# The first half of an output projection as seven half-size products, and the branch products ahead of it in another order

## What is computed

```python
y_a = diff_attention(...)                 # 256 x 512
y_b = gated_delta_net(...)                # 256 x 512
merged = (sigmoid(m_gate_a) * (y_a @ w_branch_attn)    # 512 x 1024
          + sigmoid(m_gate_b) * (y_b @ w_branch_gdn))
x = x + merged @ w_out                    # 1024 x 1024
h2 = rms_norm(x, norm_ffn_gain)
x = x + hier_moe(h2, ...)                 # 32 experts, all weights are read
return rms_norm(x, norm_final_gain)
```

## Time and profile before

| | us |
|---|---|
| median of 3 runs | 453.04 |
| lowest and highest | 451.39, 454.26 |
| the profiled execution | 453.07 |
| its span in the profile | 451.0 |
| PE busy | 421.1 (93%) |
| DVE busy | 232.8 (52%) |
| ACT busy | 129.2 (29%) |
| POOL busy | 86.1 (19%) |
| DMA traffic | 136.94 MB, mean 304 GB/s |

### The profile page before, as it was taken

One profiled execution on the slowest core, in us unless ns is written; L12 is line 12 of the kernel. 1 busy time (PEld: TensorE's weight loads), 2 busy tenths in 40 slices (PEclk: granted clock), 3 DMA queues, 4 the chain that ended last, 5 costly groups with the idle time before them and its releaser, 6 DMA issues.

```text
span 451.0 us, 11018 instructions
## 1 busy us (share of the span) xinstructions
PE 421.1 (93%) x4599; PEld 339.1 (75%) x4599; DVE 232.8 (52%) x591; ACT 129.2 (29%) x334; POOL 86.1 (19%) x126
## 2 busy tenths in 40 slices
PE   8999999999999999999999899999999797769883
PEld 8885598884899999999888786768686656437451
DVE  3376777896446478549413644445363422334033
ACT  6001622100410455331103442333242322213053
POOL 4010600000548957975000000000000000000001
PEclk9999999999999999999999999999999988998699
DMA  8979726234905045399995999999999999999982
GB/s 302 408 251 311 273 85 210 91 130 94 327 2 188 13 175 187 116 394 418 390 424 220 380 419 421 419 419 424 421 419 423 423 420 421 423 423 420 419 343 100
DMA packets 38198, 136.94 MB, mean 304 GB/s; under 512 B 8592, under 2 KB 9936, under 8 KB 26256
## 3 DMA queue, kind: packets, MB, share of 16 engines
q1 hardware_dynamic: 33808, 135.22, 75.9%
q10 hardware_dynamic: 4352, 1.21, 1.2%
HBM read 134.59 MB, written 1.84 MB: 303 GB/s over the span
## 4 chain that ended last, share of the span: by engine, by line
PE 74%; DMA 17%; DVE 4%; issue 1%; ACT 1%; SPq 1%; POOLq 0%; DVEq 0%; ACTq 0%
PE ps L1076 22%; PE ps L1122 11%; PE ps L1549 10%; PE ps L1412 6%; DMA extra<-in_moe_w_up 6%; DMA arena<-in_moe_w_up 6%; DMA arena<-in_moe_w_down 5%; PE ps L1508 4%; PE ps L1592 4%; PE ps L1602 3%; PE ps L1390 2%; PE ps L1557 1%; PE ps L1137 1%; PE ps L1024 1%; PE ps L1497 1%
## 5 line engine op out<-in xcount | busy, mean ns | idle before, releaser
L1076 PE MATMUL ps<-arena 128*128 128x256 f32 (+1 forms) x384 | 98.6, 416 | 0.0
L1076 PEld LDWEIGHTS ps<-arena 128*128 128x128 f32 x384 | 72.2, 190 | 22.3 <-issue 14.2
L1549 PE MATMUL ps<-arena 128*32 128x128 f32 x1040 | 39.9, 296 | 9.5 <-DMA arena<-in_moe_w_up 9.3
L609 POOL TENSOR_SCALAR ring<-ring,small 128x512 f32<-128x512 f32 x1 | 1.6, 1567 | 235.1 <-DVE small L2308 235.1
L1549 PEld LDWEIGHTS ps<-arena 128*32 128x32 f32 x1040 | 31.0, 115 | 16.0 <-DMA arena<-in_moe_w_up 7.8
L873 ACT ACTIVATE gains<-ps 32x256 f32<-32x256 f32 x62 | 23.3, 377 | 55.6 <-PE ps L1592 55.2
L560 POOL TENSOR_TENSOR ring<-arena 128x256 f32<-128x256 f32 x32 | 22.6, 741 | 78.0 <-DMA arena<-in_w_in 70.6
L2354 DVE TENSOR_TENSOR masks<-ps,masks 128x64 f32<-128x64 f32 x32 | 7.2, 224 | 54.0 <-ACT masks L854 53.8
L2370 DVE COPY arena<-ps 32x256 f32<-32x256 f32 x62 | 25.8, 417 | 11.1 <-PE ps L1592 10.2
L1412 PE MATMUL ps<-arena 128*128 128x256 f32 x128 | 29.1, 383 | 0.9 <-DVE arena L2220 0.9
L1549 PE MATMUL ps<-ring,arena 128*32 128x128 f32 x768 | 26.6, 277 | 3.4 <-DMA ring<-in_moe_w_up 3.4
(11 more groups left out here) (341 smaller groups left out, 622.7 us busy)
## 6 DMA issues: line engine op xcount, KB each, us to landing
arena<-in_moe_w_down SPq DMA_DIRECT2D x19, 1024.0 KB, 26.4
arena<-in_w_in SPq DMA_DIRECT2D x8, 2048.0 KB, 8.5
arena<-in_moe_w_gate SPq DMA_DIRECT2D x16, 1024.0 KB, 23.3
arena<-in_moe_w_up SPq DMA_DIRECT2D x16, 1024.0 KB, 24.2
ring<-in_moe_w_gate SPq DMA_DIRECT2D x12, 1024.0 KB, 20.4
ring<-in_moe_w_up SPq DMA_DIRECT2D x12, 1024.0 KB, 20.5
ring<-in_moe_w_down SPq DMA_DIRECT2D x12, 1024.0 KB, 21.6
arena<-in_w_out SPq DMA_DIRECT2D x2, 2048.0 KB, 9.0
```

The lines of the kernel that those rows point to most:

```text
L1076: last = pe.matmul(out, lhs, rhs, start=(k == 0 and (i > 0 or part % 2 == 0)), stop=(k == KD - 1), skip_group_check=(i == 0))
L1549: last = pe.matmul(c.ps[ROWS * q:ROWS * (q + 1), i % 2, 0:P], c.Hg[:, k, ROWS * i:ROWS * (i + 1)], w[:, :, start:start + 127:2], start=(k ...
```

## The change

`LATE` is a new order, P1, P2, P5, P6, P7, P3, P4, for `b1`; in it P4 is added on top of P7 in the bank of P1, P6 and P7 once DVE has read that bank for C22, so ACT's copy of P4 falls away. POOL makes S3 ahead of S4 for `b1`. DVE finishes `merged` in four token halves in place of two tiles: `merged_ready` counts to 4, and its last part is token half 0 of `merged[1]`, which needs P4.

A third set of seven products (j = 2) takes the place of `mix(0)` to `mix(3)`: the quarters of the first half of `w_out` (from `stage1`) times the quarters of `merged`. POOL makes its S1 to S4 (16 more instructions of 128x256, into tiles dv, cq, kdec and vn), DVE its T1 to T4 (128x512 each, into hT). P1 needs `merged[0]`, token half 0, P2 and T1 to T4 need all of `merged`. Each product is 8 matmuls of 128 columns. The results go over PSUM banks 4, 5 and 6, by ACT's copies and DVE's adds, into `x1T`, where x is added. `mix(4)` to `mix(7)` stay as they are, with the logits spread between them otherwise. On SP, expert 7 is loaded ahead of expert 4, after all four parts of `merged`; experts 4 and 5 wait for the last product of j = 2 (before: `merged` done, and half of the mixes done), expert 6 for `mix(7)`, the last one, as before.

```diff
+LATE = ("P1", "P2", "P5", "P6", "P7", "P3", "P4")
...
 def branch_done(j, product):
-    return len(ORDER) * j + ORDER.index(product) + 1
+    return len(ORDER) * j + (ORDER, LATE, LATE)[j].index(product) + 1
+
+
+def late_copied(j, product):
+    return copied("b0", "P4") + 3 * (j - 1) + ("P1", "P5", "P6").index(product) + 1
+
+
+def late_added(j, quarter):
+    return added("b0", "C2") + 3 * (j - 1) + ("C11", "C22", "C12").index(quarter) + 1
+
+
+def summed(j, form):
+    names = COMBINED if j == 0 else ("S1", "S2", "S3", "S4")
+    return combined("b0", "S1") - 4 + 16 * j + 4 * (names.index(form) + 1)
...
+    c.mixed = [v3(ap, 4) for ap in c.merged]
+    c.mix_form = {n: v3(at("hT", 512, 512 * i), 4) for i, n in enumerate(("T1", "T3", "T2", "T4"))}
+    for i in range(2):
+        for t in range(2):
+            c.mix_form[f"B{i + 1}{t + 1}"] = c.mixed[i][:, :, P * t:P * t + P]
+    c.mix_sum = {n: v3(at(place_, 1024), 4) for n, place_ in zip(COMBINED, ("dv", "cq", "kdec", "vn"))}
...
-            if e == 5:
+            if e == 4 or e == 5:
+                sp.wait_ge(s["branch_ready"], 3 * len(ORDER))
+            if e == 6:
                 sp.wait_ge(s["mix_out"], KD // 2)
-            if e == 6:
-                sp.wait_ge(s["mix_out"], KD)
...
-    sp.wait_ge(s["merged_ready"], 2)
+    sp.wait_ge(s["merged_ready"], 4)
+    load_expert(SLOTS - 1)
     load_expert(4)
-    load_expert(SLOTS - 1)
     load_expert(5)
     load_expert(6)
...
-    for j, name in enumerate(BRANCHES):
+    for j in range(3):
         i = NCH + j
-        w = branch_quarters(c, j)
+        w = branch_quarters(c, j) if j < 2 else weight_quarters(c, i)
+        sums = c.branch_sum if j < 2 else c.mix_sum
 
         def free(product):
             if j:
-                pool.wait_ge(s["branch_ready"], branch_done(0, product))
+                pool.wait_ge(s["branch_ready"], branch_done(j - 1, product))
         def combine(out, one, other, op):
-            for k in range(2):
-                for f in range(2):
-                    cols = slice(TOK * f, TOK * f + TOK)
-                    pool.tensor_tensor(c.branch_sum[out][:, k, cols], one[:, k, cols], other[:, k, cols], op).then_inc(s["forms_combined"], 1)
+            for k in range(4):
+                part = (slice(None), k, slice(None)) if j == 2 else (slice(None), k // 2, slice(TOK * (k % 2), TOK * (k % 2) + TOK))
+                pool.tensor_tensor(sums[out][part], one[part], other[part], op).then_inc(s["forms_combined"], 1)
         pool.wait_ge(s[f"stage_loaded{i % 2}"], 16 * (i // 2 + 1))
         if j == 0:
             pool.wait_ge(s["side_ready"], SI["oa1"] + 1)
         free("P5")
         combine("S1", w["A21"], w["A22"], ALU.add)
-        pool.wait_ge(s["forms_combined"], combined(name, "S1"))
+        pool.wait_ge(s["forms_combined"], summed(j, "S1"))
         if j == 0:
             pool.wait_ge(s["ya_ready"], 1)
         free("P6")
-        combine("S2", c.branch_sum["S1"], w["A11"], ALU.subtract)
-        pool.wait_ge(s["forms_combined"], combined(name, "S2"))
+        combine("S2", sums["S1"], w["A11"], ALU.subtract)
+        pool.wait_ge(s["forms_combined"], summed(j, "S2"))
+        if j > 0:
+            free("P7")
+            combine("S3", w["A11"], w["A21"], ALU.subtract)
         free("P3")
-        combine("S4", w["A12"], c.branch_sum["S2"], ALU.subtract)
-        free("P7")
-        combine("S3", w["A11"], w["A21"], ALU.subtract)
+        combine("S4", w["A12"], sums["S2"], ALU.subtract)
+        if j == 0:
+            combine("S3", w["A11"], w["A21"], ALU.subtract)
...
+    if j == 2:
+        return c.x1T[:, 2 * a:2 * a + 2, P * t:P * t + P]
...
-    return c.ps[:, BANKS[BRANCHES[j]][BANK_OF[product]], :].rearrange("p (a f) -> p a f", a=4)
+    if j == 2:
+        return c.ps[:, {"P2": 5, "P5": 6, "P3": 6}.get(product, 4), 0:TOK].rearrange("p (a f) -> p a f", a=2)
+    bank = 0 if j == 1 and product == "P4" else BANK_OF[product]
+    return c.ps[:, BANKS[BRANCHES[j]][bank], :].rearrange("p (a f) -> p a f", a=4)
...
-    copy_branch(1, "P1", "C11")
-    copy_branch(1, "P5", "C22")
-    copy_branch(1, "P6", "C12")
-    copy_branch(1, "P4", "C21")
+    for j in range(1, 3):
+        copy_branch(j, "P1", "C11")
+        copy_branch(j, "P5", "C22")
+        copy_branch(j, "P6", "C12")
...
+            forms = dict(c.mix_form, **weight_quarters(c, i), **c.mix_sum)
+        blocks, ks = ((4, 2), (4, 2), (2, 4))[j]
+        been = (lambda product: copied("b0", product)) if j == 0 else (lambda product: late_copied(j, product))
...
+            begins = product in ("P1", "P2", "P5") or (product == "P4" and j == 0)
+            if begins and j < 2:
+                branch_free(BRANCHES[j], product)
+            if j == 2 and product == "P1":
+                pe.wait_ge(s["merged_ready"], 1)
+            elif j == 2 and product == "P2":
+                pe.wait_ge(s["merged_ready"], 4)
             if product == "P6":
...
+            elif product == "P4" and j > 0:
+                pe.wait_ge(s["quarter_added"], late_added(j, "C22"))
...
+            for a in range(blocks):
+                for k in range(ks):
...
-    branch_products(1, "P1", "P2", "P5", "P6", "P4", "P3", "P7")
+    branch_products(1, *LATE)
+    branch_products(2, *LATE)
...
-    low, high = range(KD // 2), range(KD // 2, KD)
-    for ks in (low, high):
-        for b in range(3):
-            mix(b, ks)
+    mix(4, range(KD))
     logits(0)
     logits(1)
-    for b in range(3, KD):
-        mix(b, range(KD))
-        if b < KD - 1:
-            logits(b - 1)
+    mix(5, range(KD))
+    logits(2)
+    logits(3)
+    mix(6, range(KD))
+    logits(4)
+    mix(7, range(KD))
+    logits(5)
     logits(KD - 2)
     pe.wait_ge(s["squares1_added"], KD - 2)
     lengths(0)
...
     add_branch(1, "C11", "P2", "P1")
-    v.wait_ge(s["quarter_added"], added("b1", "C11"))
+    v.wait_ge(s["quarter_added"], late_added(1, "C11"))
     chain(v.tensor_tensor(tokens(g2, 0), tokens(g2, 0), branch_part(c, 1, "C11"), ALU.mult))
     settle()
-    chain(v.tensor_tensor(tokens(g2, 0), tokens(g2, 0), tokens(g0, 0), ALU.add))
-    v.wait_ge(s["product_copied"], copied("b1", "P6"))
+    v.tensor_tensor(tokens(g2, 0), tokens(g2, 0), tokens(g0, 0), ALU.add).then_inc(s["merged_ready"], 1)
+    v.wait_ge(s["product_copied"], late_copied(1, "P6"))
     early = branch_part(c, 1, "C12")
     chain(v.tensor_tensor(early, early, tokens(g2, 1), ALU.mult))
     settle()
     chain(v.tensor_tensor(early, early, tokens(g0, 1), ALU.add))
-    v.wait_ge(s["product_copied"], copied("b1", "P4"))
-    low = flat_half(1, 1)
-    chain(v.tensor_tensor(low, low, g3, ALU.mult))
+    add_branch(1, "C22", "P7", "P5")
+    v.wait_ge(s["quarter_added"], late_added(1, "C22"))
+    chain(v.tensor_tensor(tokens(g3, 1), tokens(g3, 1), branch_part(c, 1, "C22"), ALU.mult))
+    settle()
+    v.tensor_tensor(tokens(c.merged[1], 1), tokens(g3, 1), tokens(g1, 1), ALU.add).then_inc(s["merged_ready"], 1)
     v.wait_ge(s["branch_ready"], branch_done(1, "P3"))
     v.tensor_tensor(tokens(g2, 1), tokens(g2, 1), branch_out(c, 1, "P3"), ALU.mult).then_inc(s["quarter_added"], 1)
     settle()
-    v.wait_ge(s["quarter_added"], added("b1", "C12"))
+    v.wait_ge(s["quarter_added"], late_added(1, "C12"))
     v.tensor_tensor(tokens(g2, 1), tokens(g2, 1), early, ALU.add).then_inc(s["merged_ready"], 1)
-    chain(v.tensor_tensor(low, low, g1, ALU.add))
-    v.wait_ge(s["branch_ready"], branch_done(1, "P7"))
-    gate3 = g3.rearrange("p (a j f) -> p a j f", a=4, j=2)
-    v.tensor_tensor(gate3, gate3, both_tokens(1), ALU.mult).then_inc(s["quarter_added"], 1)
-    settle()
-    v.wait_ge(s["quarter_added"], added("b1", "C2"))
-    v.tensor_tensor(c.merged[1], low, g3, ALU.add).then_inc(s["merged_ready"], 1)
+    v.wait_ge(s["branch_ready"], branch_done(1, "P4"))
+    chain(v.tensor_tensor(tokens(g3, 0), tokens(g3, 0), branch_out(c, 1, "P4"), ALU.mult))
+    settle()
+    v.tensor_tensor(tokens(c.merged[1], 0), tokens(g3, 0), tokens(g1, 0), ALU.add).then_inc(s["merged_ready"], 1)
+
+    f = c.mix_form
+    v.wait_ge(s["merged_ready"], 3)
+    v.tensor_tensor(f["T1"], f["B12"], f["B11"], ALU.subtract).then_inc(s["branch_forms"], 1)
+    v.tensor_tensor(f["T3"], f["B22"], f["B12"], ALU.subtract).then_inc(s["branch_forms"], 1)
+    v.wait_ge(s["branch_forms"], branch_formed(2, "T1"))
+    v.tensor_tensor(f["T2"], f["B22"], f["T1"], ALU.subtract).then_inc(s["branch_forms"], 1)
+    v.wait_ge(s["branch_forms"], branch_formed(2, "T2"))
+    v.wait_ge(s["merged_ready"], 4)
+    v.tensor_tensor(f["T4"], f["B21"], f["T2"], ALU.subtract).then_inc(s["branch_forms"], 1)
...
-    for b in range(KD):
-        v.wait_ge(s["mix_out"], b + 1)
-        v.tensor_tensor(c.x1T[:, b, :], c.xT[:, b, :], mix_out(c, b), ALU.add).then_inc(s["x1T_ready"], 1)
-        if 1 <= b < KD - 1:
+    def add_x(quarter):
+
+        a, t = int(quarter[1]) - 1, int(quarter[2]) - 1
```

(57 more changed lines are left out.)

## The result

| | before | changed |
|---|---|---|
| median, 20 runs each | 452.71 us | 454.92 us |
| lowest, highest | 451.39, 455.05 | 453.14, 456.23 |
| ratio, 95% interval | | 1.0041 (1.003 to 1.0052) |
| profiled execution, its span | 453.07, 451.0 | 455.44, 453.6 |

The forecast was +2.4 us (455.4). The medians differ by 2.2 us; the ratio, which is not that of the medians, gives 1.9 us, with an interval from 1.4 to 2.4. In the profiled executions the span grew by 2.6 us. Expert 6 was issued 1.98 us later there, of which 0.24 us were there before the changed code began (ACT's copy of P6 in `b1` starts at 207.35 in place of 207.11 us). So the change itself moved the last mix by 1.74 us in the profile. The times alone can't tell 1.74 us from 2.4; what else counts is read from the traces: expert 8, in a place that the prediction had called covered.

The account below looks back on a forecast made before the run. The expert weight stream was taken to end the kernel, started by the last mix on PE. PE savings of -1.59, -0.85 and -0.37 against waits of +0.79, +0.57, +1.05, +2.73 and +0.1 gave +2.4 us: 455.4, own range 454.3 to 456.4.

Parts of the forecast that it names:

- the end moves with the end of the last mix ... microsecond for microsecond: Expert weight stream: its end follows `mix(7)` on PE, as long as experts queued ahead of expert 6 are through.
- a DMA hole behind 250 us: Transfers: DMA holes after 250 us were listed among the signs that the forecast is wrong; no size given.
- wait for `merged` gone: PE at 213.29 us: the wait falls away, as the third set's P1 needs only a quarter long ready; -0.85 us.
- PE's own work, logits step: PE: four mixes go and seven products come, -1.59 us; `logits(5)` moves behind `mix(7)`, -0.37 us for expert 6.
- P7 of `b1` behind the copy: PE in `b1`: P7 directly behind P6 waits for ACT's copy of P6; +0.79 us.
- P4 behind C22: PE in `b1`: P4 waits for DVE's add for C22, delayed by operations slowed beside POOL; +1.05 us.
- P2 behind the last part: PE in the third set: P2 waits for part 4 of `merged` from DVE, slowed beside POOL; +2.73 us.
- P7 of the third set behind the copy: PE in the third set: P7 waits for ACT's 128x256 copy; +0.57 us.
- +4.4: DVE beside POOL: total in us if each of six two-SBUF-input operations were blocked for a whole POOL instruction, 0.73 us.
- DVE not slowed: Rival, chance 0.2: DVE stays near its free pitch beside POOL; -0.7 us, 452.3 us.
- The clock falls: Rival, chance 0.2: PE's clock halves after the wait ahead of the third set's P2; 1.6 us more, 457.0 us.
- The transfers take over: Rival, chance 0.1: slow transfers of experts 4 and 5, or late POOL sums; +0.5 to +2 on the forecast.

Follow-up runs that it names:

- x4: The changed kernel with 8 useless matmuls on PE right ahead of expert 0's first matmul; ratio to the kernel before 1.008 (1.0052 to 1.0108).
- x12: The kernel before with 8 useless matmuls on PE right ahead of expert 0's first matmul; ratio 1.0023 (1.0 to 1.0045).
- x11: The changed kernel with P3 ahead of P7 in `b1` and S4 ahead of S3 again; ratio to the kernel before 1.003 (1.0009 to 1.0052).
- x1: The changed kernel with POOL's 16 sums of the third set 1 column wide instead of 256; ratio to the kernel before 1.0006 (0.9984 to 1.0027).
- x2: The changed kernel with each third-set POOL sum split into two instructions of 128 columns; ratio to the kernel before 1.0093 (1.0064 to 1.0122).
- x3: The kernel before with only the new order of `b1` and DVE's merge in four parts; ratio 1.0008 (0.9992 to 1.0025).

## Why the prediction was right, point by point

**What sets the end.** Right in the large: the stream of expert weights ends last, and its start moves with PE. Too narrow in one step: "the end moves with the end of the last mix ... microsecond for microsecond", with the logits step called covered. x4 and x12 show a second release, expert 8's, by estimate 0.5 us behind in the kernel before and level with it in the changed one. One of the prediction's own signs of being wrong, a DMA hole behind 250 us, came true at 258 to 261 us. That the total came out near is in part luck: the last mix moved less than forecast, 1.74 us, and expert 8's release, by the logits step and by the clock's fall in the routing, moved more.

**The sum for the last mix.** From the end of P6 in `b1` to expert 6's issue the kernel before took 243.86 - 207.11 = 36.75 us, the changed one 245.84 - 207.35 = 38.49, so +1.74 us. Measured from start to start:

| term | predicted | measured |
|---|---|---|
| wait for `merged` gone | -0.85 | -0.82 |
| PE's own work, logits step | -1.96 | -1.83 |
| P7 of `b1` behind the copy | +0.79 | +0.65 |
| P4 behind C22 | +1.05 | +0.97 |
| P2 behind the last part | +2.73 | +1.93 |
| P6 behind T2 | +0.1 | 0 |
| P7 of the third set behind the copy | +0.57 | +0.74 |
| start of `mix(4)` | 0 | +0.10 |
| sum | +2.4 | +1.74 |

The rows say where PE stood still, not what each is worth alone: x11 shows that without the wait behind the copy the one behind C22 grows.

The mis-sized term is the wait ahead of P2, 0.8 us too large. The price of a DVE operation beside POOL was taken as 0.51 us for each of six; it was 0.52, 0.41, 0.50, 0.41, 0.43 and 0, which is 0.8 us less in all. One row had been taken for all, with 1.10 beside it in the same group. The bounds of 0 and a POOL instruction held.

**The whole-instruction rule.** The Trainium skill (SBUF — State Buffer, "SBUF: two separate sides") says that whichever of the two starts first holds the shared ports for its whole instruction and the other is blocked. x1 and x2 agree in kind: no POOL sums, no price; halved pieces, 0.83 us in place of 2.27. The +4.4 read this as a whole POOL instruction for every operation. The page sets a whole one as the most, not as the price of each, and an operation never paid all of the 0.73 us here, so the +4.4 did not come.

**SP and the transfers.** Right: the hole at 226 to 232 us, experts 4 and 5 at 229.8 (forecast 230.2), full transfers from 232 to 246 us, and a short hole ahead of expert 6. POOL was done at 225.34 us, 0.3 later than its range and 0.6 ahead of its need.

**The rivals.** *DVE not slowed*: it fell with the rows, and x1 shows what it would have been, the last mix at 243.65 us and a ratio of 1.0006 (0.9984 to 1.0027), no gain that can be seen. *The clock falls*: not at the wait ahead of P2, 1.7 us long in its row; a fall did come, in the routing behind a wait of 1.45 us, which the kernel before has too. *The transfers take over*: not by experts 4 and 5, but that another release can bind beside the last mix was sound, at expert 8.

**What stays open.** Why the clock falls in the routing in some profiles and not in others with the same waits. Whether x3's 1 us at the last mix is fully paid in time. Whether the time moved by more than the last mix's share, which the interval of 1.4 to 2.4 us leaves open. And how the loss divides between the two releases in the mean over executions; only single changes of each were measured. Taking POOL's reads out of DVE's way without lengthening POOL's work was not tried.

## What to carry to other kernels

An edit that saves columns on the matmul engine must be priced with the sums it hands to other engines: here 1.6 us saved on PE put 16 POOL instructions beside a DVE chain on the path, and they cost 2.1 us of waits (x1), on top of those for copies and for the chain itself. Where transfers set the end, look for every release that starts a piece of the stream and how much queued work stands between it and the next; the tightest two count, and a step "moved behind" one of them lands ahead of the other. Waits on one chain are not additive: take one away and see whether the next grows.

## What the runs showed of the hardware

- A VectorE operation of 128x512 float32 with two SBUF inputs took 0.68 to 0.70 us alone and mostly 1.10 to 1.21 beside GpSimd sums of 128x256 (0.73 us each), 0.83 to 0.99 beside sums of 128x128, though some operations beside either still took 0.69; with one input in PSUM it took 0.67 to 0.68 in all cases.
- GpSimd's sums were stretched as well: in the changed kernel the 48 of them had a mean duration of 0.91 us, a median of 0.78 and a least of 0.72.
- A sum of half the columns cost GpSimd 0.41 us from start to start in place of 0.73, so by estimate about 0.1 us of each does not shrink.
- The granted clock stayed at 1.00 through a wait of 1.67 us between the products. In the routing it was 0.50 for 3 us behind a wait of 1.45 us in the changed kernel, and stayed at 1.00 behind the same wait of 1.44 us in x11.
